# Attention stages of a two-block transformer kernel: half a key piece ahead of the up products, two piece rows ahead of the scores, waits for value copies moved to the values, and four output low halves on GpSimd

## What is computed

```python
h = rmsnorm(x, ln1_g[i]) @ w_in[i]
(fq, fk, fv, ff, dq, dk, dv, c_q, c_kv, k_r) = jnp.split(h, split_points, axis=-1)
o_fox = fox_group(fq, fk, fv, ff, fgate_b[i])
o_diff = diff_group(dq, dk, dv, lam_q1[i], ..., diff_norm_g[i], lam_init)
o_mla = mla_group(c_q, c_kv, k_r, q_norm_g[i], w_uq[i], kv_norm_g[i], w_ukv[i], pos)
x = x + jnp.concatenate([o_fox, o_diff, o_mla], axis=-1) @ w_o[i]
```

## Time and profile before

| what | value |
|---|---|
| median of three runs | 2614.44 us |
| lowest and highest | 2613.68 and 2616.26 us |
| the profiled execution | 2616.33 us |
| its span from first to last instruction | 2615.1 us |
| TensorE busy in it | 2562.8 us (98%) |
| VectorE, ScalarE, GpSimd busy | 1133.2, 914.3, 356.7 us |
| mean granted clock of TensorE | 0.996 of full |

### The profile page before, as it was taken

One profiled execution on the slowest core, in us unless ns is written; L12 is line 12 of the kernel. 1 busy time (PEld: TensorE's weight loads), 2 busy tenths in 40 slices (PEclk: granted clock), 3 DMA queues, 4 the chain that ended last, 5 costly groups with the idle time before them and its releaser, 6 DMA issues.

```text
span 2615.1 us, 32699 instructions
## 1 busy us (share of the span) xinstructions
PE 2562.8 (98%) x13324; PEld 1789.3 (68%) x13324; DVE 1133.2 (43%) x1971; ACT 914.3 (35%) x1741; POOL 356.7 (14%) x160
## 2 busy tenths in 40 slices
PE   9999999999999999999989999999999999999999
PEld 7874444444777444445477778888888767888887
DVE  2543233323685233223353453552554344465264
ACT  4431111111484111111164454442345454443233
POOL 2200000000340000000030011231222002222212
PEclk9999999999999999999999999999999999999999
DMA  6248999999325999999921112232232112223222
GB/s 219 83 193 356 421 421 420 421 421 420 113 97 214 412 420 422 421 421 421 407 80 59 55 65 81 97 108 86 65 117 71 62 33 81 75 87 124 78 65 80
DMA packets 133367, 542.23 MB, mean 207 GB/s; under 512 B 13024, under 2 KB 24672, under 8 KB 84064
## 3 DMA queue, kind: packets, MB, share of 16 engines
q1 hardware_dynamic: 129264, 536.94, 52.5%
q10 hardware_dynamic: 3952, 3.17, 0.4%
HBM read 537.98 MB, written 2.10 MB: 207 GB/s over the span
## 4 chain that ended last, share of the span: by engine, by line
PE 91%; DVE 4%; DMA 2%; ACT 2%; issue 1%; POOL 0%; SPq 0%; POOLq 0%; DVEq 0%; ACTq 0%
PE ps L622 21%; PE ps L1516 16%; PE ps L624 15%; PE ps L1538 8%; PE ps L646 5%; PE ps L1492 4%; PE ps L555 4%; PE ps L2132 3%; PE ps L1553 2%; PE ps L1554 2%; DMA w<-in_moe_w_up 2%; PE ps L2089 2%; PE ps L2120 2%; PE ps L556 1%; PE ps L2111 1%
## 5 line engine op out<-in xcount | busy, mean ns | idle before, releaser
L283 POOL TENSOR_TENSOR w<-w,w 128x1024 fp32r<-128x1024 f32 (+2 forms) x136 | 335.2, 2474 | 2206.3 <-ACT w L275 2202.1
L622 PE MATMUL ps<-w,w 128*128 128x512 f32 x2592 | 590.7, 389 | 2.6 <-POOL w L283 2.6
L622 PEld LDWEIGHTS ps<-w,w 128*128 128x128 f32 x2592 | 486.1, 188 | 104.8 <-POOL w L283 3.4
L1516 PE MATMUL ps<-w,w 128*64 128x512 f32 x2048 | 445.4, 592 | 3.5 <-issue 2.0
L624 PE MATMUL ps<-w,w 128*128 128x512 f32 (+1 forms) x1872 | 408.8, 379 | 5.3 <-DVE w L541 3.0
L624 PEld LDWEIGHTS ps<-w,w 128*128 128x128 f32 x1872 | 337.9, 188 | 72.6 <-issue 5.9
L275 ACT ACTIVATE w<-w 128x1024 fp32r<-128x1024 f32 (+2 forms) x260 | 251.5, 999 | 348.9 <-PE ps L624 177.9
L283 DVE TENSOR_TENSOR w<-w,w 128x1024 fp32r<-128x1024 f32 (+2 forms) x124 | 200.8, 1626 | 350.6 <-ACT w L275 348.1
L1516 PEld LDWEIGHTS ps<-w,w 128*64 128x64 f32 x2048 | 149.0, 137 | 293.6 <-issue 293.6
L1538 PE MATMUL ps<-w,w 128*64 128x512 f32 x1024 | 226.8, 595 | 0.8 <-ACT w L1614 0.8
L1764 DVE TENSOR_TENSOR w<-ps,w 128x512 f32<-128x512 f32 x32 | 34.7, 1083 | 388.8 <-PE ps L1516 388.8
(11 more groups left out here) (257 smaller groups left out, 2471.4 us busy)
## 6 DMA issues: line engine op xcount, KB each, us to landing
w<-in_moe_w_gate SPq DMA_DIRECT2D x128, 1024.0 KB, 15.6
w<-in_moe_w_up SPq DMA_DIRECT2D x128, 1024.0 KB, 18.5
w<-in_moe_w_down SPq DMA_DIRECT2D x128, 1024.0 KB, 15.0
w<-in_w_up SPq DMA_DIRECT2D x40, 1024.0 KB, 5.1
w<-in_w_down SPq DMA_DIRECT2D x20, 1024.0 KB, 5.2
w<-in_w_in SPq DMA_DIRECT2D x16, 1024.0 KB, 5.2
w<-in_ab_w_in SPq DMA_DIRECT2D x10, 1024.0 KB, 7.6
w<-in_c_w_in SPq DMA_DIRECT2D x8, 1024.0 KB, 7.8
```

What stands on the lines that cost most here:

```text
L283: up(self.wlo[self.low[s][0]], lane.e.tensor_tensor(lo, raw, hi.bitcast(F32), ALU.subtract))
L622: ins = pe.matmul(bank[:, :], wp[:, k, P * o:P * o + P], ap(k0 + k), start=first, stop=stop)
L1516: ins = pe.matmul(bank[64 * e:64 * e + 64, :], XG[p % 3][:, 4 * u + k, 64 * e:64 * e + 64], w[e][:, k, :], start=(u == 0 and k == 0), stop ...
```

## The change

- In front of the up products, half a `dk` piece is done (`piece(0, range(KD // 2), first_keys)`, twelve matmuls into bank 7); its other half follows behind the gate sums. Meanwhile the up products take their banks from 0 to 6.
- In front of the first scores, and in front of the waits for the copies of queries and keys, the first two row blocks of piece 2 are done (six matmuls); step 0 then does none.
- The waits for the copied values behind `dv` and `fv` are dropped there and stand in `tensor_values`, in front of the first `diff` values and the first `fox` values.
- The halves of the first 512 output columns (24 to 27) all get their lows from GpSimd (`pool=True`); before, 24 and 26 were VectorE's. This moves two lows in each attention.

```diff
--- before.py
+++ after.py
@@ -34,7 +34,7 @@
 NOVER = T // CAP - 1
 TAIL = 4
 ALL_BANKS, SCORE_BANKS, OTHER_BANKS = tuple(range(8)), (0, 1, 2, 3), (4, 5, 6, 7)
-TURN_BANKS, PIECE_BANK = (4, 5, 6), (7,)
+TURN_BANKS, PIECE_BANK, UP_BANKS = (4, 5, 6), (7,), (0, 1, 2, 3, 4, 5, 6)
 BLOCKS = (3, 1, 2, 0)
 
 PACK = [
@@ -193,7 +193,7 @@
         self.ring_start = -NSPLIT
         self.low, self.n_low = [], [0, 0]
 
-    def add(self, key, parts, split=True, expert=False):
+    def add(self, key, parts, split=True, expert=False, pool=False):
         parts = [(k, cols, src if isinstance(src, tuple) else ((0, cols, src),)) for k, cols, src in parts]
         if expert:
             slot = self.ring[self.n_expert % NRING]
@@ -210,7 +210,7 @@
             for h in range(2):
                 s = len(self.halves)
                 self.halves.append((u, h))
-                engine = int(s % 2 == 1 or s < self.ring_start + NSPLIT)
+                engine = int(pool or s % 2 == 1 or s < self.ring_start + NSPLIT)
                 self.n_low[engine] += 1
                 self.low.append((engine, self.n_low[engine]))
                 self.half_earlier.append(self.holder[NRAW + s % NSPLIT])
@@ -583,13 +583,13 @@
 
 
 
-    def plan_cols(key, w, c0, n, order=(0, 1)):
+    def plan_cols(key, w, c0, n, order=(0, 1), pool=False):
         for u in order:
-            W.add(key, [(4, n, w[512 * u:512 * u + 512, c0:c0 + n].rearrange("(k p) n -> p k n", p=P))])
-
-    def plan_out(key, w, order=(0, 1)):
+            W.add(key, [(4, n, w[512 * u:512 * u + 512, c0:c0 + n].rearrange("(k p) n -> p k n", p=P))], pool=pool)
+
+    def plan_out(key, w, order=(0, 1), pool=False):
         for n in range(2):
-            plan_cols((key, n), w, 512 * n, 512, order)
+            plan_cols((key, n), w, 512 * n, 512, order, pool=pool and n == 0)
 
     def tensor_product(key, outs, width, a, kind, ready=None, feature=False, between=None, tail=0, ahead=None,
                        amid=None):
@@ -1979,7 +1979,7 @@
                           (1, 512, A["w_ukv_2"][i].rearrange("(k p) n -> p k n", p=P))], split=False)
         for key, c0, n in (("dk", 1284, 512), ("dv", 1796, 512), ("fqk", 0, 512), ("fv", 512, 256)):
             plan_cols((key, i), w, c0, n)
-        plan_out(("atto", i), A["w_o_2"][i], OUT_ORDER)
+        plan_out(("atto", i), A["w_o_2"][i], OUT_ORDER, pool=True)
 
     def attention(i, rows, late, last_square, last_norm, next_rows):
         H, (HTH, HTL), ahead = rows.H, (rows.hi, rows.lo), i > 0
@@ -2112,6 +2112,8 @@
                 up(bpt.full, ins)
 
         def tensor_values(m, two):
+            if two[0][1] != "mla":
+                PE.wait_ge(ba.free, 10 + 8 + 4 + 1 + (4 if two[0][1] == "diff0" else 8))
             for m, (qc, _, _, _, _, vals, dv) in turned_jobs(m, two):
                 n = turn_of(m)
                 PE.wait_ge(bpt.free, n + 1)
@@ -2150,6 +2152,9 @@
             tensor_product(("dq", i), ALL4, 512, H, ba, feature=True)
             PE.wait_ge(ckv, 8)
             tensor_features(lambda c, k: CM[:, c, P * k:P * k + P], 3, lambda k: bv if k % 2 else ba)
+            piece, first_keys = tensor_pieces(("dk", i)), banks.take(bpc, PIECE_BANK)
+            banks.among = UP_BANKS
+            piece(0, range(KD // 2), first_keys)
             PE.wait_dma(W.s_raw[up_unit.slot], up_unit.arrived)
             raw = W.raw[up_unit.slot]
             wq = raw[:, 0:768].rearrange("p (k n) -> p k n", k=2)
@@ -2170,14 +2175,12 @@
                     ins = pe.matmul(bank[:, 4 * c:4 * c + 4], cst("trii") if j == c else cst("ones"), LF[:, j, :],
                                     start=(j == 0), stop=(j == c))
             up(bv.full, ins)
-            piece = tensor_pieces(("dk", i))
-            for o in (0, 1):
-                piece(o, range(KD), banks.take(bpc))
+            piece(0, range(KD // 2, KD), first_keys)
+            banks.among = ALL_BANKS
+            piece(1, range(KD), banks.take(bpc))
             PE.wait_ge(q1k1, 1)
             tensor_features(lambda c, h: Q1[:, c, 96 * h:96 * h + 96], 4, lambda k: bv if k % 2 else ba, rows=96)
             tensor_features(lambda c, h: K1[:, c, h, :], 4, lambda k: bv if k % 2 else ba, rows=96)
-            PE.wait_ge(ba.free, 10 + 8 + 4)
-            PE.wait_ge(bv.free, 2 + 4)
             open_piece = {}
 
             def sums_turned():
@@ -2197,7 +2200,7 @@
 
             def tensor_between(m, two):
                 p = m // 2
-                if p < DIFF_STEP:
+                if p < DIFF_STEP and p:
                     done = piece_rows(piece, 2 + p // 4, range(2 * (p % 4), 2 * (p % 4) + 2))
                     if p == DIFF_STEP - 1:
                         consume(("dk", i), done)
@@ -2221,7 +2224,6 @@
                 tensor_product(("dv", i), ALL4, 512, H, ba)
                 banks.among = TURN_BANKS
                 queries.append(tensor_pieces(("fqk", i)))
-                PE.wait_ge(ba.free, 10 + 8 + 4 + 1 + 4)
 
             def queries_of_fox():
                 piece_rows(queries[0], 2, range(KD), TURN_BANKS)
@@ -2231,8 +2233,10 @@
             def values_of_fox():
                 banks.among = OTHER_BANKS
                 tensor_product(("fv", i), ALL4, 256, H, ba)
-                PE.wait_ge(ba.free, 10 + 8 + 4 + 1 + 4 + 4)
             PE.wait_ge(bpc.free, 2)
+            piece_rows(piece, 2, range(2))
+            PE.wait_ge(ba.free, 10 + 8 + 4)
+            PE.wait_ge(bv.free, 2 + 4)
             banks.among = TURN_BANKS
             mark["o"] = len(bf.banks)
             pipeline(engine, with_features({1: sums_turned, DV_STEP: values_of_diff, FOX_STEP: queries_of_fox,
```

## The result

The change made the kernel slower: a median of 2621.42 us over 12 executions (2617.8 to 2623.89) against 2614.64 us over 12 of before. The ratio is 1.0026, with a 95% interval of 1.0018 to 1.0033, so 4.7 to 8.6 us more, 6.8 by the middle. The forecast was 2617.4 us and no change that can be measured. The time lies inside the range, but the slowdown can be told from no change; the number is the third rival's, 2621.4 us.

A forecast was written before the change was run, and what follows sets the result against it. TensorE, busy 98% of the span, was taken to bound the kernel, so only its waits could give time. -3.0 - 0.6 - 1.4 - 0.2 + 8.2 = +3.0 us gave 2617.4 us on the median, range 2611.5 to 2623.

The forecast's parts named there:

- third rival: Behind `fv`: the clock falls behind TensorE's new stop, up to 1.7 us each; +7 us in all, 2621.4 us; chance 16%.
- Half a piece: Ahead of the up products: twelve matmuls cover the 1.52 us gap; gain 1.5 us in each attention, 3.0 us.
- Two row blocks: Ahead of the first scores: 0.87 us gap filled, new 0.6 us wait at step 2; gain 0.3 us each, 0.6 us.
- Waits at the values: Behind `dv`: 0.69 us of idle goes in each attention, gain 1.4 us; nothing counted for the wait behind `fv`.
- the 0.47 us: The dropped wait of TensorE behind `fv`; counted as no gain, because VectorE's later maximum stops TensorE next.
- Lows on GpSimd: `fv` step: five lows beside VectorE's norm instead of two, maximum 4.1 us later; loss 4.1 us each attention, 8.2 us.
- first rival: `fv` step: VectorE keeps its place and GpSimd's lows wait, norm 7 us or less; -10 us, 2604 us; chance 13%.
- the second (low 29 stays behind): `fv` step: only the two moved GpSimd lows come in beside the norm; -1.2 us, 2613 us; chance 10%.
- The stop of 4.7 us: TensorE's predicted new idle stretch behind `fv`, at the value product that needs a bank VectorE frees behind its maximum.
- That 3.0: Whole kernel: the predicted sum of all parts, +3.0 us, without any clock cost behind the new stop.
- the second part's gain: The 0.6 us predicted for the two row blocks ahead of the first scores, which one rival counted as nothing.

The follow-up runs named there:

- e4_stop_filled: The change plus 36 idle matmuls in each attention, in TensorE's stop behind `fv`, against before: 2617.3 us, ratio 1.0014.
- e1_no_pool: The change without its fourth part, lows 24 and 26 staying on VectorE, against before: 2611.13 us, ratio 0.9988.

## Why the prediction was right or wrong, step by step

- **Half a piece: right, a little undersized.** 3.0 us were predicted; the gap of 1.52 us is filled in each attention. With the clock alike in both kernels the part is worth 1.7 us each, 3.4 us, and alone it measured 3.7 us with an interval that holds both numbers.
- **Two row blocks: right in the new wait, undersized in the gain.** 0.6 us of wait were predicted and 0.57 came; the gain was 0.46 us each instead of 0.3, within the bounds. What the prediction did not see is that this part rests on the first: alone, it waits for the bank of the last key.
- **Waits at the values: right.** The 0.69 us went, and counting nothing for the 0.47 us was right: alone they came back, in the first attention as 0.63 us behind VectorE's maximum.
- **Lows on GpSimd: the mechanism right, to 0.1 us.** Five lows beside the norm, five instructions of 2.4 to 2.5 us, 6.3 us more where 6.4 were predicted. From the start of the norm to the maximum it is 16.76 us instead of 12.77, so 4.0 us where 4.1 were predicted, and a stop of 4.63 us where 4.7 were (3.93 in the second attention). The first rival (VectorE keeps its place, a norm of 7 us) and the second (low 29 stays behind) fell: all five lows came in, one directly behind the other. The Trainium skill (SBUF — State Buffer, Who interferes with whom) says that a VectorE instruction with two SBUF inputs contends with a GpSimd instruction that reads SBUF; the norms of 5.07, 9.43 and 15.70 us agree with that.
- **The step that failed is the clock.** The text put it so: "Behind it TensorE has pauses of 1.10 and 0.56 us that hide a part, so I take none of it for the likeliest sum". The half-clock stretches came behind both stops, and the pauses hid only a part: from the value product behind the stop to the next one but one it is 10.32 us in the first attention (before 9.59) and 10.74 in the second (before 9.13), 0.7 and 1.6 us. The third half-clock stretch, at 1569.93, cost about 1.5 us more, but it does not need a stop: the row blocks alone have one like it there, 3.41 us, and take 63.00 us from `fv` to the output product in that attention and 61.47 in the other. Over many executions the clock cost more than in this profile: with the stop filled the kernel is 3.1 to 4.1 us faster, although it does more. The stop of 4.7 us was nearly as long as the one of 5.50 us in the earlier trace rows, behind which the clock had fallen; the text said so, and gave it 16%.
- **That 3.0 and these 3 to 4 us make the 6.8 measured is in part luck.** The starts of the same instructions in the two profiles give this account of the first and the second attention, in us:

| from, to (TensorE) | before | the change |
|---|---|---|
| first turned feature, first turned query | 26.43, 26.42 | 23.11, 23.14 |
| on to the scores of step 2 | 10.40, 10.40 | 9.94, 9.94 |
| on to the first matmul of `fv` | 113.48, 113.49 | 112.79, 112.80 |
| on to the first matmul of the output product | 61.45, 61.43 | 67.43, 66.27 |

The rows for the last line in the first attention, two of before and two of the change:

```profile
1517.53 12.29 PE L624 MATMUL ps<-w,w 128*128 128x256 f32 x96
...
1578.98 16.49 PE L646 MATMUL ps<-w,w 128*128 128x512 f32 x72
```

```profile
1514.78 12.30 PE L624 MATMUL ps<-w,w 128*128 128x256 f32 x96
...
1582.21 16.49 PE L646 MATMUL ps<-w,w 128*128 128x512 f32 x72
```

The two attentions together are 1.9 us longer. Another 1.7 us lie ahead of the first, where only the profile of the change has 3.41 us at half clock (from 672.2 us on), and 0.1 us less behind the second: 3.5 us between the two profiles. In the first line 1.6 us each are the clock again, lost by before alone. Without any half-clock stretch the parts come to some 2 us more than before. This is an estimate from profiles without such a stretch at the place. In front and at the end 3.4 + 0.9 + 1.4 + 0.1 us are gained. From `fv` on 4.1 us are lost in each attention (65.11 us in the second attention of e4_stop_filled, 61.05 in that of e1_no_pool), and the half piece gains 0.4 there in the second (alone 61.08, before 61.43). So the clock makes, on balance, some 5 of the 6.8 us, rather than 3 to 4.

- **The third rival's number was right for a reason that was half wrong:** it added 3.4 us for the clock, which cost more, and took the second part's gain away. That gain was there.

Two things stay open. What lets the clock fall behind `fv` in some executions without the lows was not settled: directly behind `fv`, neither the waits alone nor the row blocks alone showed it in their profiles, and the half piece alone had one short stretch there. The profiles do show a pattern. Of the 24 attentions in the twelve profiles, eight have a half-clock stretch behind the gate sums, and none of these has one between `fv` and the output product; of the other sixteen, nine have. So an execution that is spared the one may meet the other; the cause is open. And why a low waits behind three VectorE lows in one place and gets in between two norm instructions in the other was not tried.

## What to carry to other kernels

A lightly used engine is no free place for work: the two engines shared a resource here, and each low on GpSimd cost VectorE 2.1 to 2.2 us where doing it itself would have cost 1.14, at the one place where TensorE waits for VectorE. When a sum leaves a stop of several us on TensorE, the clock behind it belongs in the likeliest sum if the trace has shown the clock fall behind a stop of like length; read what the same instructions take behind it. Before the difference of two profiles is put down to an edit, the half-clock stretches of both have to be laid side by side: here before lost 1.6 us in each attention at a place where the change lost nothing, and the change 1.7 us at a place that it does not touch. And when three edits are made together, ask of each which bank, buffer or wait it finds as the others left it.

## What was not expected of the hardware

- **Idle work made the program faster.** 36 matmuls into a bank about to be overwritten, in a stop of 4.6 us, gave 3 to 4 us by the medians, with higher mean clocks in the executions. The profile shows TensorE's clock kept up behind the second stop, worth 1.2 us; the fall behind the first is half as long, which gained nothing by the end of that stretch.
- **The clock can fall behind short pauses too, in some executions and not in others of the same kernel:** with idle stretches of 0.63 and 1.09 us there was no fall in one profile and 6.83 and 10.24 us at half clock in two others, worth 2.3 and 3.9 us. The mean granted clock of an execution goes with its time: where it was 0.997 the kernel without the lows took 2607 to 2609 us, where it was 0.994 about 2613.6.
